# Shifted copies of a gated input for a 31-tap convolution: sixteen copies inside the core's memory a tile, or one store to device memory and four overlapping loads

## The chip, the cores and the metric

One core of one Trainium2 chip runs the whole program. Its engines are PE (TensorE, matrix products), DVE (VectorE), ACT (ScalarE), POOL (GpSimd) and SP (SyncE), each with its own queue, worked off in order; sixteen DMA engines move data for all of them. The metric is the device time of one execution in microseconds (us), lower is better.

## The reference

Two blocks follow each other: a conformer-like block with a recurrent branch and a pooling block, then a second block with chunked linear attention and a feed-forward part. Sequence length is 256, the width 1024, all in 32-bit floats. The change lies in the first block's convolution branch alone:

```python
def conformer_conv(va, vg, p):
    u = va * jax.nn.sigmoid(vg)
    u = depthwise_conv(u, p["conv_w"], p["conv_b"], CONV_PAD)      # 31 taps, padded 15 on each side
    return jax.nn.silu(layernorm(u, p["ln_g"], p["ln_b"]))

def even_mixer(h, h0, p):
    z = h @ p["w_in"]
    va, vg, ga, xb, gb = jnp.split(z, [W_CONV, 2 * W_CONV, 3 * W_CONV, 3 * W_CONV + W_LRU], axis=-1)
    y_a = conformer_conv(va, vg, p) * jax.nn.silu(ga)
    y_b, hT = rglru_branch(xb, p, h0, True)
    y_b = y_b * jax.nn.silu(gb)
    return jnp.concatenate([y_a, y_b], axis=-1) @ p["w_out"], hT
```

## The kernel before

Channels lie on the 128 partitions and time (256 steps) along the free dimension, so a tensor of width 1024 is eight tiles. All weights come as one stream of 512 KB tiles, in the order that `ORDER` lists (lines 49 to 74). A tile passes four stations. SP loads it into one of six buffers `raw` (L414), and to load tile n it waits until PE is done with tile n - 6. ACT rounds it to a high part `w_hi` (L866). DVE makes the rest, `w_lo` (L1230). PE multiplies in three products per 128 rows (L505 to L507), 24 instructions a tile. The tiles `gate` (recurrent gates) and `cv` (convolution) are used as they come, without ACT and DVE. ACT and DVE prepare weights at fixed places of their programs: ACT's `done(name, t)` first rounds everything up to four tiles ahead, and then waits for the named tile.

A second stream, `modw`, brings the modulation weights, 80 tiles of 512 KB, issued from POOL (L446) whenever DVE has used one of four buffers (L1264).

The stretch of the change is the first block's middle. For t = 0 to 7 PE makes `va t` and `vg t`; ACT copies `va` into the padded buffer `upad` (L919, three buffers) and writes the sigmoid of `vg` to `sg` (L924); DVE multiplies them in `gated(t)` (L1383). The convolution's 31 taps are then done on PE (L573) as 8 groups of 4 taps: the contraction runs over 32 channels times 4 taps. For that `shifts` (two buffers) has to hold, for each of four channel groups g, the 32 channels four times, on partitions 32 s to 32 s + 31 shifted by s steps. Between them PE runs the gates of the recurrent branch, `gates(head)` (L562). PE's order, with pieces of about equal weight, is: va 0, vg 0, gates 0, va 1, vg 1, gates 1, va 2, vg 2, conv 0, va 3, vg 3, conv 1, gates 2, va 4, vg 4, gates 3, conv 2, va 5, vg 5, conv 3, gates 4, va 6, vg 6, gates 5, conv 4, va 7, vg 7, conv 5, ga 0, ga 1, conv 6, gates 6, ga 2, ga 3, gates 7, conv 7, ga 4 to ga 7, statistics. In the order of the weight stream one `gate` tile serves two heads: gate 1 (heads 2 and 3) stands after vg 4, gate 2 after vg 6, gate 3 after ga 3.

ACT has one more thing to do here: `exps_of(p)` (L958, L962), twelve instructions on end for two heads, during which it rounds no weights. SP's queue interleaves the shifted copies with the weight stream: after the weight tile n is issued, and if tile n - 6 is a `vg t`, the sixteen copies of t follow, and only then the next weight tile.

Of the kernel before, what the change touches and what calls it, by code (L numbers as in the profile page):

```python
# [19 lines left out]
F32 = mybir.dt.float32  # L20
# [5 lines left out]
P = 128  # L26
D = 1024
T = 256
KT = D // P
RING = 6  # L30
# [18 lines left out]
def tiles_in_order():  # L49
    order = [("xb", t) for t in range(KT)]  # L50
    order += [("va", 0), ("vg", 0), ("va", 1), ("vg", 1), ("gate", 0), ("va", 2), ("vg", 2), ("cv", 0)]
    order += [("va", 3), ("vg", 3), ("cv", 1), ("va", 4), ("vg", 4), ("gate", 1), ("cv", 2)]
    order += [("va", 5), ("vg", 5), ("cv", 3), ("va", 6), ("vg", 6), ("gate", 2), ("cv", 4)]
    order += [("va", 7), ("vg", 7), ("cv", 5), ("ga", 0), ("ga", 1), ("cv", 6), ("ga", 2), ("ga", 3), ("gate", 3)]
    order += [("cv", 7)] + [("ga", t) for t in range(4, KT)] + [("gb", t) for t in range(KT)]
    for m in range(0, KT, 4):
        order += [("ya", t) for t in range(m, m + 4)] + [("yb", t) for t in range(m, m + 4)]
    order += [("ou", t) for t in range(2 * KT)] + [("og", t) for t in range(2 * KT)]
    order += [("grp", t) for t in range(KT)]
    for m in range(0, KT, 4):  # L60
        order += [("oa", t) for t in range(m, m + 4)] + [("ob", t) for t in range(m, m + 4)]
    order += [("f", t) for t in range(2 * HEADS)] + [("i", t) for t in range(HEADS)] + [("q", t) for t in range(HEADS)]
    order += [(n, t) for n in ("u", "v", "o") for t in range(HEADS)]
    order += [(n, t) for n in ("ga2", "gb2") for t in range(KT)]
    order += [(n, t) for t in range(HEADS) for n in ("pa", "pb")]
    order += [("wo", t) for t in range(KT)]
    order += [(n, t) for t in range(FT) for n in ("ua", "ub")]
    order += [(n, t) for t in range(KT) for n in ("d0", "d1", "d2")]
    return order


ORDER = tiles_in_order()
# [79 lines left out]
def build(nc, ins, out):  # L152
    with ExitStack() as ctx:
        base = nc.sbuf_base + (-nc.sbuf_base) % 32

        def at(name, kib, shape, dt=F32):
            return nc.alloc_sbuf_tensor_at(name, [P] + shape, dt, offset=base + int(kib * 1024))

        def sem(name):
            return ctx.enter_context(nc.semaphore(name))  # L160
# [27 lines left out]
        def columns(n):  # L188

            used[0] += n  # L190
            assert used[0] <= 448
            return small[:, used[0] - n:used[0]]
# [16 lines left out]
        UW = T + CONV_TAPS + 1  # L209
        RW = T + CONV_TAPS - 3  # L210
        shifts = [at("shifts0", W + 16, [4, RW]), at("shifts1", W + 32, [4, RW])]
        sg = at("sg", W + 20.5, [3, T])
        upad = at("upad", W + 36.5, [3, UW])
# [102 lines left out]
        h_ready = sem("h_ready")  # L316
        u_ready = sem("u_ready")
        u_gated = sem("u_gated")
        shifts_in = [sem(f"shifts_in{j}") for j in range(2)]
        ya_raw, ya_rounded, ya_ready = sem("ya_raw"), sem("ya_rounded"), sem("ya_ready")  # L320
        yb_raw, yb_rounded, yb_ready = sem("yb_raw"), sem("yb_rounded"), sem("yb_ready")
# [49 lines left out]
        lb_t = [columns(2 * HEADS) for _ in range(3)]  # L371
        lb, oml, noml = (columns(2 * HEADS) for _ in range(3))

        block = ctx.enter_context(nc.Block())


        def psum_of(name, t):

            return ps[PLACE[(name, t)][0]]
# [6 lines left out]
        def free_of(name, t):  # L386

            return ps_free[PLACE[(name, t)][0]]


        @block.sync
        def _(sp):
            sp.dma_start(ccs, ins["c_cols"]).then_inc(in_cc, 16)
            sp.dma_start(ctxT[:], ins["ctxT"]).then_inc(in_ctx, 16)
            sp.dma_start(x[:], ins["xT"]).then_inc(in_x, 16)
            sp.dma_start(cols[:], ins["cols"]).then_inc(in_con, 16)
            for k in range(KT):
                sp.dma_start(m0[:, k, :], ins["mod0_w"][k]).then_inc(mod0_in[k], 16)

            def shifted_copies(t):  # L400

                sp.wait_ge(u_gated, t + 1)
                if t >= 2:
                    sp.wait_ge(tile_done, TILE[("cv", t - 2)] + 1)
                for g in range(4):
                    for s in range(4):
                        sp.dma_start(shifts[t % 2][32 * s:32 * s + 32, g, :],  # L407
                                     upad[32 * g:32 * g + 32, t % 3, s:s + RW]).then_inc(shifts_in[t % 2], 16)

            def weights(first, end):  # L410
                for n in range(first, end):
                    if n >= RING:
                        sp.wait_ge(tile_done, n - RING + 1)
                    sp.dma_start(raw[n % RING][:], ins["stream"][n]).then_inc(raw_in[n % RING], 16)  # L414
                    if n >= RING and ORDER[n - RING][0] == "vg":
                        shifted_copies(ORDER[n - RING][1])

            weights(0, 4)
            sp.dma_start(con[:], ins["con"]).then_inc(in_con2, 16)
            sp.dma_start(c_row[:, 1, :], ins["c_rows"][0:1, :].partition_broadcast(P)).then_inc(in_crow, 16)  # L420
            weights(4, TILE[("ou", 0)] + RING)
            sp.wait_ge(prod_ready, KT)
            for n in (1, 2):
                sp.dma_start(c_row[:, 2 * n - 2, :], ins["c_rows"][n:n + 1, :].partition_broadcast(P)).then_inc(in_crow2, 16)
            weights(TILE[("ou", 0)] + RING, TILE[("og", 0)] + RING)
            sp.dma_start(ctx2T[:], ins["ctx2T"]).then_inc(in_ctx2, 16)
            weights(TILE[("og", 0)] + RING, TILE[("f", 0)] + RING)
            sp.dma_start(wsT[:], ins["wsT"]).then_inc(in_sgu, 16)
            sp.dma_start(bsr[0:1, :], ins["b_s"]).then_inc(in_sgu, 16)
            sp.dma_start(tri[:], ins["tri"]).then_inc(in_sgu, 16)  # L430
            weights(TILE[("f", 0)] + RING, NTILES)
            for k in range(KT):
                sp.wait_ge(stored, k + 1)
                sp.dma_start(out[:, k, :], x[:, k, :]).then_inc(out_done, 16)
            sp.wait_ge(out_done, 16 * KT)
# [14 lines left out]
        def _(pe):  # L450
# [22 lines left out]
            def weights(name, t):  # L473

                n = TILE[(name, t)]
                pe.wait_ge(raw_in[n % RING], 16 * (n // RING + 1))
                return raw[n % RING]

            def bank_of(name, t):

                bank, before = PLACE[(name, t)]
                if before:
                    pe.wait_ge(ps_free[bank], before)
                return ps[bank]
# [81 lines left out]
            def convolve(t):  # L566

                w, o = weights("cv", t), bank_of("cv", t)
                pe.wait_ge(shifts_in[t % 2], 256 * (t // 2 + 1))
                for n in range(QUADS):  # L570
                    for g in range(4):
                        c = slice(32 * g, 32 * g + 32)
                        mm = pe.matmul(o[c, 0:T], w[:, n, c], shifts[t % 2][:, g, 4 * n:4 * n + T], start=(n == 0),  # L573
                                       stop=(n == QUADS - 1))
                mm.then_inc(tile_done, 1)
# [8 lines left out]
            gates(1)  # L584
            va_vg(2)
            convolve(0)
            va_vg(3)
            convolve(1)
            gates(2)
            va_vg(4)  # L590
            gates(3)
            convolve(2)
            va_vg(5)
            convolve(3)
# [259 lines left out]
        def _(act):  # L854
# [14 lines left out]
            def done(name, t):  # L869

                highs(*ORDER[min(TILE[(name, t)] + RING - 2, NTILES - 1)])
                act.wait_ge(tile_done, TILE[(name, t)] + 1)
# [42 lines left out]
            def va_vg_out(t):  # L915
                done("va", t)
                if t >= 3:
                    act.wait_ge(shifts_in[(t - 3) % 2], 256 * ((t - 3) // 2 + 1))
                act.activation(upad[:, t % 3, CONV_LEFT:CONV_LEFT + T], psum_of("va", t)[:, 0:T], ACT.Copy) \  # L919
                   .then_inc(free_of("va", t), 1)  # L920
                done("vg", t)
                if t >= 3:
                    act.wait_ge(u_gated, t - 2)
                act.activation(sg[:, t % 3, :], psum_of("vg", t)[:, 0:T], ACT.Sigmoid).then_inc(free_of("vg", t), 1)  # L924
# [39 lines left out]
            def roots(p):  # L964
                for head in (2 * p, 2 * p + 1):
                    act.wait_ge(prod_ready, head + 1)
                    r = lr[:, PAIR_BUF[p] + head % 2]
                    act.activation(r, r, ACT.Sqrt).then_inc(root_ready, 1)

            va_vg_out(0)  # L970
            sigmoids(0)
            va_vg_out(1)
            sigmoids(1)
            va_vg_out(2)
            exps_of(0)
            conv_out(0)
# [1029 lines left out]
```

## Time and profile before

| | us |
|---|---|
| median of 3 runs | 1072.86 |
| lowest, highest | 1071.97, 1073.68 |
| the profiled execution | 1070.74 |
| its span, first to last instruction | 1068.9 |
| PE busy | 938.7 (88%) |
| PE weight loads busy | 867.8 (81%) |
| DVE busy | 709.9 (66%) |
| ACT busy | 503.7 (47%) |
| DMA: mean rate | 183 GB/s |
| shifted copies: issues, KB each | 128, 35.5 |

The busy shares are averages over the whole span. The stretch in which the shifted copies are issued runs from about 90 to 214 us, and the rows further down are read there. A stall is the idle time of an engine just before an instruction, and the profile names what ended it.

### The profile page before, as it was taken

Reading aid. Unit: us, or ns where it says so; the run is one execution under the profiler, and the core shown is the slowest. Engines: PE = TensorE matmul, PEld = TensorE weight load, DVE = VectorE, ACT = ScalarE, POOL = GpSimd, SP = SyncE. Lnnn points to the kernel's source line nnn. Section 1 sums busy time; section 2 is a strip of 40 time slices with the busy share of each in tenths; the row PEclk is TensorE's granted clock in tenths of the full one; section 3 lists DMA queues with packets and bytes.
Section 4 is the critical chain, followed back from the end, with each engine's and each line's share of the span. In section 5 each row is a group of like instructions: output and inputs, shape, how many; then the busy total and the mean of one; then the engine's idle time right before and its main releaser. Section 6 shows DMA issues by size and latency. Waiting matters only on the chain.

```text
span 1068.9 us, 17178 instructions
## 1 busy us (share of the span) xinstructions
PE 938.7 (88%) x7056; PEld 867.8 (81%) x7056; DVE 709.9 (66%) x1057; ACT 503.7 (47%) x725; POOL 42.5 (4%) x84
## 2 busy tenths in 40 slices
PE   5799698587799899897997898986989979999996
PEld 3588465457799899886997898986979979999996
DVE  3986647745955599977748796545458587566553
ACT  3634766667645554225334356446242445444441
POOL 0001000100000000100001200000000000000000
PEclk9799898798899899998999898997988989999998
DMA  9737756752456368874724954432334646666661
GB/s 378 287 103 222 243 171 227 254 193 82 119 178 195 140 182 289 286 248 141 275 94 180 356 177 121 132 118 60 99 99 123 177 156 202 189 180 181 194 201 57
DMA packets 57920, 195.27 MB, mean 183 GB/s; under 512 B 7921, under 2 KB 13169, under 8 KB 56434
## 3 DMA queue, kind: packets, MB, share of 16 engines
q1 hardware_dynamic: 46322, 152.23, 44.1%
q0 software_dynamic: 11520, 41.95, 11.5%
q8 instruction: 56, 0.92, 0.4%
q14 instruction: 22, 0.18, 0.0%
HBM read 188.44 MB, written 1.05 MB: 177 GB/s over the span
## 4 chain that ended last, share of the span: by engine, by line
PE 53%; DVE 19%; DMA 11%; ACT 7%; SPq 6%; issue 4%; DVEq 0%; ACTq 0%
PE ps L505 15%; PE ps L506 14%; PE ps L507 14%; SPq L407 6%; DVE w_lo L1230 5%; DMA raw<-in_stream 5%; DMA modw<-in_mod_w 4%; PE px L562 3%; ACT w_hi L866 2%; DMA m<-in_mod_w 2%; DVE modw L1264 2%; PE px L469 2%; DVE dump L1585 1%; DVE t L1250 1%; PE ps L573 1%
## 5 line engine op out<-in xcount | busy, mean ns | idle before, releaser
L1230 DVE TENSOR_TENSOR w_lo<-raw,w_hi 128x1024 fp32r<-128x1024 f32 x232 | 280.1, 1223 | 181.0 <-ACT w_hi L866 180.5
L866 ACT ACTIVATE w_hi<-raw 128x1024 fp32r<-128x1024 f32 x232 | 243.5, 1055 | 170.5 <-DMA raw<-in_stream 170.4
L505 PE MATMUL ps<-h_hi,w_hi 128*128 128x256 f32 (+1 forms) x928 | 280.3, 302 | 44.7 <-DVE w_lo L1230 29.6
L506 PE MATMUL ps<-h_lo,w_hi 128*128 128x256 f32 (+1 forms) x928 | 275.2, 297 | 0.0
L507 PE MATMUL ps<-h_hi,w_lo 128*128 128x256 f32 (+1 forms) x928 | 275.0, 296 | 0.0
L505 PEld LDWEIGHTS ps<-h_hi,w_hi 128*128 128x128 f32 x928 | 183.9, 198 | 54.8 <-DVE w_lo L1230 35.6
L506 PEld LDWEIGHTS ps<-h_lo,w_hi 128*128 128x128 f32 x928 | 184.0, 198 | 3.9 <-issue 1.2
L507 PEld LDWEIGHTS ps<-h_hi,w_lo 128*128 128x128 f32 x928 | 183.5, 198 | 2.6
L505 PE MATMUL ps<-h2o_hi,w_hi 128*128 128x256 f32 x352 | 107.0, 304 | 29.4 <-DVE w_lo L1230 13.0
L507 PE MATMUL ps<-h2o_hi,w_lo 128*128 128x256 f32 x352 | 104.1, 296 | 0.0
L506 PE MATMUL ps<-h2o_lo,w_hi 128*128 128x256 f32 x352 | 104.0, 296 | 0.0
L505 PEld LDWEIGHTS ps<-h2o_hi,w_hi 128*128 128x128 f32 x352 | 72.1, 205 | 32.0 <-DVE w_lo L1230 14.0
L1264 DVE SCALAR_TENSOR_TENSOR modw<-modw,c_row 128x1024 f32<-128x1024 f32 x64 | 76.2, 1223 | 16.9 <-DMA modw<-in_mod_w 16.8
L446 POOL DMA_DIRECT2D modw<-in_mod_w x80 | 42.3, 530 | 829.5 <-DVE modw L1264 557.8
L506 PEld LDWEIGHTS ps<-h2o_lo,w_hi 128*128 128x128 f32 x352 | 72.2, 205 | 0.3 <-issue 0.2
L507 PEld LDWEIGHTS ps<-h2o_hi,w_lo 128*128 128x128 f32 x352 | 72.1, 205 | 0.0
L562 PE MATMUL px<-xpad,raw 128*128 128x512 f32 x64 | 35.1, 699 | 17.4 <-DMA raw<-in_stream 17.4
L505 PE MATMUL ps<-ff_hi,w_hi 128*128 128x256 f32 x176 | 49.8, 283 | 0.0
L506 PE MATMUL ps<-ff_lo,w_hi 128*128 128x256 f32 x176 | 49.8, 283 | 0.0
L507 PE MATMUL ps<-ff_hi,w_lo 128*128 128x256 f32 x176 | 49.8, 283 | 0.0
L1041 ACT ACTIVATE sq<-x 128x256 f32<-128x256 f32 x32 | 13.4, 417 | 74.2 <-DVE x L1538 74.2
L562 PEld LDWEIGHTS px<-xpad,raw 128*128 128x128 f32 x64 | 13.8, 226 | 34.2 <-DMA raw<-in_stream 18.9
(301 smaller groups left out, 1730.8 us busy)
## 6 DMA issues: line engine op xcount, KB each, us to landing
raw<-in_stream SPq DMA_DIRECT2D x252, 512.0 KB, 3.7
modw<-in_mod_w POOLq DMA_DIRECT2D x80, 512.0 KB, 6.0
m<-in_mod_w SPq DMA_DIRECT2D x8, 1024.0 KB, 16.2
shifts<-upad SPq DMA_DIRECT2D x128, 35.5 KB, 3.7
c_row<-in_c_rows SPq DMA_DIRECT2D x3, 512.0 KB, 6.5
ctxT<-in_ctxT SPq DMA_DIRECT2D x1, 1024.0 KB, 4.9
x<-in_xT SPq DMA_DIRECT2D x1, 1024.0 KB, 7.0
ctx2T<-in_ctx2T SPq DMA_DIRECT2D x1, 1024.0 KB, 6.8
```

What stands on the lines that cost most here:

```text
L407: sp.dma_start(shifts[t % 2][32 * s:32 * s + 32, g, :], upad[32 * g:32 * g + 32, t % 3, s:s + RW]).then_inc(shifts_in[t % 2], 16)
L446: pool.dma_start(modw[j][:], ins["mod_w"][t]).then_inc(modw_in[j], 16)
L469: last = pe.matmul(bank[:, 0:T], ones, squares(k), start=(k == 0), stop=(k == tiles - 1))
L505: pe.matmul(o, wh, hi, start=start, stop=False)
L506: pe.matmul(o, wh, lo, start=False, stop=False)
L507: return pe.matmul(o, wl, hi, start=False, stop=stop)
L562: mm = pe.matmul(px[b][:, :], w[:, 4 * e + b, :], xpad[:, head, :, SCONV_LEFT:SCONV_LEFT + T], start=True, stop=True)
L573: mm = pe.matmul(o[c, 0:T], w[:, n, c], shifts[t % 2][:, g, 4 * n:4 * n + T], start=(n == 0), stop=(n == QUADS - 1))
L866: act.activation(w_hi[split[0] % HI_RING][:], raw[n % RING][:], ACT.Copy).then_inc(w_hi_ready, 1)
L1041: act.activation(dst[:, t, :], x[:, t, :], ACT.Square).then_inc(sq_ready, 1)
L1230: v.tensor_tensor(w_lo[n % RING][:], raw[n % RING][:], w_hi[split[0] % HI_RING][:].bitcast(F32), ALU.subtract).then_inc(w_lo_ready, 1)
L1264: v.scalar_tensor_tensor(out=modw[s][:], in0=modw[s][:], scalar=1.0, in1=c_row[:, row, :], op0=ALU.mult, op1=ALU.mult, accum_out=mod[:, t: ...
```

## The change

For each tile t the gated input is stored once, from `upad` to a new tensor `u_rows` in device memory, 128 rows of 288 values. Four loads then fill `shifts`: load g writes all 128 partitions of group g from a source pattern that counts 4 shifts (step 1 element), 32 rows (step 288) and 284 elements. The store stands on SP's queue where the sixteen copies stood. The loads stand two weight tiles later and wait for the store's landing, and as before for the convolution that read the buffer last. PE waits for 64 instead of 256 on the landing semaphore. ACT, before it overwrites an `upad` buffer, now waits for the store and not for the shifted copies. Bytes read per tile stay at 16 x 35.5 KB; 144 KB of store are added.

```diff
+            def store_u(t):
+
+                sp.wait_ge(u_gated, t + 1)
+                sp.dma_start(u_rows.ap()[t], upad[:, t % 3, :]).then_inc(u_stored[t], 16)
+
             def shifted_copies(t):
 
-                sp.wait_ge(u_gated, t + 1)
+                sp.wait_ge(u_stored[t], 16)
                 if t >= 2:
                     sp.wait_ge(tile_done, TILE[("cv", t - 2)] + 1)
                 for g in range(4):
-                    for s in range(4):
-                        sp.dma_start(shifts[t % 2][32 * s:32 * s + 32, g, :],
-                                     upad[32 * g:32 * g + 32, t % 3, s:s + RW]).then_inc(shifts_in[t % 2], 16)
+                    sp.dma_start(shifts[t % 2][:, g, :],
+                                 bass.AP(u_rows, (t * P + 32 * g) * UW, [[1, 4], [UW, 32], [1, RW]])) \
+                      .then_inc(shifts_in[t % 2], 16)
...
                     if n >= RING and ORDER[n - RING][0] == "vg":
-                        shifted_copies(ORDER[n - RING][1])
+                        store_u(ORDER[n - RING][1])
+                    if n >= RING + 2 and ORDER[n - RING - 2][0] == "vg":
+                        shifted_copies(ORDER[n - RING - 2][1])
...
-                pe.wait_ge(shifts_in[t % 2], 256 * (t // 2 + 1))
+                pe.wait_ge(shifts_in[t % 2], 64 * (t // 2 + 1))
...
                 if t >= 3:
-                    act.wait_ge(shifts_in[(t - 3) % 2], 256 * ((t - 3) // 2 + 1))
+                    act.wait_ge(u_stored[t - 3], 16)
```

SP's queue before, at the copies of tiles 0 and 1 (`raw` are weight tiles, the number after it the buffer):

```order
L407 DMA shifts_97<-upad 32x284 [waits u_gated]
L407 DMA shifts_97<-upad 32x284 x15
L414 DMA raw_53<-in_stream 128x1024 [waits tile_done]
L414 DMA raw_54<-in_stream 128x1024 [waits tile_done]
L407 DMA shifts_98<-upad 32x284 [waits u_gated]
L407 DMA shifts_98<-upad 32x284 x15
L414 DMA raw_49<-in_stream 128x1024 [waits tile_done]
L414 DMA raw_50<-in_stream 128x1024 [waits tile_done]
```

The same place of SP's queue after the change:

```order
L406 DMA u_rows<-upad 128x288 [waits u_gated]
L422 DMA raw_53<-in_stream 128x1024 [waits tile_done]
L422 DMA raw_54<-in_stream 128x1024 [waits tile_done]
L406 DMA u_rows<-upad 128x288 [waits u_gated]
L414 DMA shifts_97<-u_rows 128x1x284 [waits u_stored0]
L414 DMA shifts_97<-u_rows 128x1x284 x3
L422 DMA raw_49<-in_stream 128x1024 [waits tile_done]
```

The loads of tile 0 have moved behind two weight tiles and behind the store of tile 1, which waits for `gated(1)`.

SP's queue before, at the copies of tile 3 and what stands around them:

```order
L414 DMA raw_54<-in_stream 128x1024 [waits tile_done]
L407 DMA shifts_98<-upad 32x284 [waits tile_done,u_gated]
L407 DMA shifts_98<-upad 32x284 x15
L414 DMA raw_49<-in_stream 128x1024 [waits tile_done]
L414 DMA raw_50<-in_stream 128x1024 [waits tile_done]
L414 DMA raw_51<-in_stream 128x1024 [waits tile_done]
L407 DMA shifts_97<-upad 32x284 [waits tile_done,u_gated]
```

And after, from the store of tile 3 to the store of tile 4:

```order
L406 DMA u_rows<-upad 128x288 [waits u_gated]
L422 DMA raw_49<-in_stream 128x1024 [waits tile_done]
L422 DMA raw_50<-in_stream 128x1024 [waits tile_done]
L414 DMA shifts_98<-u_rows 128x1x284 [waits tile_done,u_stored3]
L414 DMA shifts_98<-u_rows 128x1x284 x3
L422 DMA raw_51<-in_stream 128x1024 [waits tile_done]
L406 DMA u_rows<-upad 128x288 [waits u_gated]
```

The weight tiles for gate 1 (stream number 21) and gate 2 (28), which stood right behind a block of sixteen copies, now stand ahead of the loads of their turn; right behind a block of loads stand now, among others, va 6 (number 26, here `raw_51`) and ga 0 (33). The order of PE, ACT and DVE is unchanged.

## Rows read from the trace of the kernel before

**Rows 1.** Page, shares of the chain that ended last, by engine
```profile
PE 53%; DVE 19%; DMA 11%; ACT 7%; SPq 6%; issue 4%; DVEq 0%; ACTq 0%
```

**Rows 2.** PE in order of time: start, us, line, operation [idle before, releaser]
```profile
98.51 3.60 PE L562 MATMUL px<-xpad,raw 128*128 128x512 f32 x8
107.79 0.42 PE L573 MATMUL ps<-shifts,raw 128*32 128x256 f32 x4
129.67 1.22 PE L562 MATMUL px<-xpad,raw 128*128 128x512 f32 x1 [8.10 <-DMA raw<-in_stream]
164.41 1.22 PE L562 MATMUL px<-xpad,raw 128*128 128x512 f32 x1 [6.35 <-DMA raw<-in_stream]
205.04 0.58 PE L505 MATMUL ps<-h_hi,w_hi 128*128 128x256 f32 x1 [11.77 <-DVE w_lo L1230]
219.55 1.97 PE L562 MATMUL px<-xpad,raw 128*128 128x512 f32 x2 [2.99 <-DMA raw<-in_stream]
252.24 0.58 PE L505 MATMUL ps<-h_hi,w_hi 128*128 128x256 f32 x1 [5.69 <-DVE w_lo L1230]
```

**Rows 3.** SP's DMA issues in order of time, 90 to 214 us: start, us
```profile
90.71 10.19 SPq L407 DMA_DIRECT2D shifts<-upad  x16
100.94 1.05 SPq L414 DMA_DIRECT2D raw<-in_stream  x2
114.71 10.93 SPq L407 DMA_DIRECT2D shifts<-upad  x16
125.68 1.53 SPq L414 DMA_DIRECT2D raw<-in_stream  x3
193.85 2.82 SPq L414 DMA_DIRECT2D raw<-in_stream  x4
```

**Rows 4.** Chain that ended last, 60 to 270 us: pieces, start and us
```profile
129.67 6.01 PE px L562 x8
141.42 3.44 PE px L562 x8
144.86 3.63 PE ps L573 x64
```

**Rows 5.** Instructions on `shifts`: duration of an issue, min/median/max ns; then landing
```profile
L407 SPq DMA_DIRECT2D shifts<-upad x128: 507/591/1318, 90.7 to 213.3; - x128
DMA to landing us min/median/max: 1.8/3.7/6.3
```

**Rows 6.** By stretch: us, PE, PEld, DVE, ACT, POOL busy, PEclk, DMA share, GB/s
```profile
100.00:110.00 10.00, 10.00 (x97) 7.80 (x99) 5.42 (x9) 4.73 (x8) 2.11 (x4) 1.00 1.04 342
120.00:130.00 10.00, 1.90 (x33) 0.99 (x24) 6.35 (x8) 8.56 (x11) 0.00 (x0) 0.71 0.44 128
180.00:190.00 10.00, 9.24 (x112) 7.57 (x108) 7.83 (x13) 8.90 (x13) 2.11 (x4) 1.00 0.97 365
```

**Rows 7.** Landing of the weight tiles `raw` issued from 95 to 240 us
```profile
DMA to landing us min/median/max: 3.5/5.9/9.4
```

**Rows 8.** ACT and DVE in order of time: start, us, operation [idle before, releaser]
```profile
106.36 1.06 ACT L866 ACTIVATE w_hi<-raw 128x1024 fp32r<-128x1024 f32 x1 [3.52 <-DMA raw<-in_stream]
149.80 1.06 ACT L866 ACTIVATE w_hi<-raw 128x1024 fp32r<-128x1024 f32 x1 [0.75 <-DMA raw<-in_stream]
158.95 1.33 ACT L962 ACTIVATE lr<-lr,small 128x512 f32<-128x512 f32 x2
99.19 0.43 DVE L1383 TENSOR_TENSOR upad<-upad,sg 128x256 f32<-128x256 f32 x1 [2.80 <-ACT sg L924]
166.60 2.35 DVE L1230 TENSOR_TENSOR w_lo<-raw,w_hi 128x1024 fp32r<-128x1024 f32 x2
```

**Rows 9.** POOL's issues of modulation tiles: start, us [idle before, releaser]
```profile
102.19 0.53 POOL L446 DMA_DIRECT2D modw<-in_mod_w  x1 [4.98 <-DVE modw L1264]
178.29 0.53 POOL L446 DMA_DIRECT2D modw<-in_mod_w  x1 [38.09 <-DVE modw L1264]
```

## What the change does to the time: the prediction

> **What bounds the kernel now.** First the page's chain: over the whole span PE holds 53% of it, and SP's queue 6%, an odd place for a queue that only issues [rows 1]. The copies are all issued between 90 and 214 us, so the rest is read there. Second, PE in order of time: up to 107.79 us it does not pause, and conv 0 starts then with no wait. Then come five stalls of more than 1 us, of 8.10, 6.35, 11.77, 2.99 and 5.69 us, 34.9 together [rows 2]. Third, SP's own order: a block of sixteen copies takes 10.2 to 10.9 us of issuing, eight blocks in all, and the next weight tile goes out only then [rows 3]. The two views fit: gate 1 goes out at 125.68, behind the block of 114.71 [rows 3], and PE starts on it at 129.67 [rows 2]. The stalls of 6.35 and 2.99 are gate 2 and gate 3 in the same position. The stall of 11.77 ends by way of DVE, but starts the same way: ga 1, first behind the block of tile 6, goes out at 193.85 [rows 3]; ACT has to round it before the sigmoid of vg 7, and DVE gates before it makes ga 0's low part. So SP's issuing sets the pace in four of five stalls. Each also costs clock: the granted clock falls from 1.00 to 0.71 in the stretch of the first [rows 6], which is part of the time at 1.2 GHz and not 2.4, and the gates after it take 6.01 us where they take 3.44 at full clock [rows 4]. About 2 us more for each of five stalls.
>
> **What is removed.** Sixteen issues of 0.63 us (10.19/16, median 0.59 alone) [rows 3, 5] become a store and four loads: 5 x 0.63 = 3.2 us. SP gains 7 us eight times, 55 us in all, but only stalls count. Heads 2, 4 and 6 no longer wait for a gate tile right behind the block; the three gate tiles now stand ahead of the loads of their turn: minus 8.10, 6.35 and 2.99, **-17.4 us**.
>
> **What is added, and what one tile's loads cost the DMA engines.** No row shows a store of this kind here; its landing lies between that of a copy, 1.8 us at best, and a weight tile's 5.9 in the middle [rows 5, 7]. Two weight tiles stand between it and the loads, each issued when PE is done with a tile, 2.92 us apart (va 2 and vg 2 run from 98.51 + 3.44 to 107.79 [rows 2, 4]), so the landing is covered by 5.8 us, at nothing; with no cover it would be 1.8 to 5.9 us a tile. SP's wait for the gated input stands where it stood. ACT's wait for the store comes due earlier than the one it replaces: nothing.
>
> The loads are the dispute. No row shows a load whose two sides count differently; each old copy has 32 rows on both sides and lands in 1.8 to 6.3 us [rows 5]. The new source counts 4, then 32, then 284; the target counts 128. I take it that a transfer is dealt out over the DMA engines by the outer count of both sides, which only 4 divides here, so that four of the sixteen engines carry all four loads, while every weight tile needs all sixteen. The price comes from rows: with all engines busy they move 342 GB/s (share 1.04) or 365 GB/s (share 0.97) [rows 6], 20.6 to 23.5 GB/s each. A load has 145 KB, 36.4 KB an engine, 1.55 to 1.77 us; four take **6.2 to 7.1 us** of those four engines, against 1.6 to 1.7 spread over all. A weight tile behind them waits that long.
>
> The Trainium skill, DMA: Bandwidth & Descriptors, section "Why a DMA increments its semaphore by 16 and not by 1", says the number of engines is the largest up to 16 that divides both patterns' slowest counts, and that the lowest-numbered are used: four here, the same four each time. No row of this case shows it. The same page's "Rules for kernel authors" would have small transfers coalesced, since under 64 KB one mostly pays overhead; by that alone the change would do what the first rival says.
>
> **Conv 0.** The lead was large: copies from 90.71, conv at 107.79. Now the store of tile 1 stands ahead, and waits for gated(1), 99.19 + 0.43 [rows 8], so the loads go out from 99.7. At that place the engines are full (share 1.04 for 10 us [rows 6]); a weight tile issued at 100.94 is taken up at 106.36 [rows 3, 8], 5.4 us against 3.5 at best [rows 7]. Landing is at least 99.7 + 5.4 + 6.2 = 111.3, 3.5 late. POOL issues four modulation tiles from 102.19 [rows 9]; 512 KB each, 32 KB an engine, about 1.5 us, served between the loads: up to 6 us more; with two weight tiles still in the backlog, 3 us, some 14 late. I take **+11**, near the upper end, because nothing on those engines is idle there.
>
> **Later convolutions.** The loads of t go out when the second tile after vg t is done. To conv t that leaves PE's work in between, with 2.9 us a weight tile, 3.6 a convolution and 3.44 gates [rows 4]: 12 us for t = 1, 19 for 2, 16 for 3, 22 for 4, 16 for 5, 15 for 6, 19 for 7. The landing needs 3.5 + 6.6 = 10 us alone, and as much as 22 with eight modulation tiles in between, which POOL issues from 178.29 on [rows 9], eight within 14 us, at t = 5. So conv 5 is some 8 us late, conv 3 about 1: **+9**, between 0 and 14.
>
> **Weight tiles behind the loads.** va 6 is right behind the loads of 3. Before, it was rounded at 149.80 after 0.75 us of waiting [rows 8], so it has no slack. ACT's exponentials follow at once and end at 160.3 (158.95 + 1.33), then the next tile's rounding, the sigmoid, the gating, and only at 166.60 comes DVE's low part of va 6 [rows 8]. A tile later by 6.6 us (11 with modulation tiles) moves this whole chain. Without the stall at 164.41 PE would want va 6 at 164.41 - 6.35 + 3.6 = 161.7 [rows 2, 4], and the chain without waiting gives about 165: 3.3 + 6.6 = 9.9 at least, less the 1 us lost at conv 3: **+9**. ga 0, behind the loads of 5, is in that place again; its 11.77 stays, take **-1**. At the last stall, of 5.69, the same happens in small: **+3**. Clock: five long stalls before, five after (conv 0, va 6, conv 5, ga 0, ga 7), so 0, within 4.
>
> **Sum.** -17.4 + 11 + 9 + 9 - 1 + 3 = +13.6. Against the profiled execution, 1070.74, that is 1084.3; against the median shown, 2.1 above it, 1086.4. Forecast **1086 us**, by itself between 1080 and 1093.
>
> **Rival 1, the loads spread over all sixteen engines** (or the source is dealt out by rows). Then four loads take 1.7 us and block nobody. For it: every row of a transfer here shows wide spreading. Against it: none of those has a source like this one. The 17.4 goes; conv 0 is still late by the moved issue, about 5 (111.3 - 6.2 + 1.7 = 106.8, plus modulation tiles); the exponentials on ACT, 9 us without rounding, leave va 6 a new stall of 5 (3.3 by the chain above, and a landing 2 later) and ga 0 one of 5 in place of 11.77; four long stalls and not five cost 2 us less clock: -17.4 + 5 + 5 - 6.8 - 2 = -16: 1057, from 1048 to 1066. It decides from the point where a block of loads costs a weight tile behind it less than the 7 us that SP saves.
>
> **Rival 2, the four engines are slower still.** The sources start at odd elements, 1136 bytes long, and between two queues a short piece may be served in turn with a 4 KB one. At 9 us a block and not 6.6, each of conv 0, conv 3, va 6, conv 5 and ga 0 loses 2.4 more: +12: 1098, to 1104.
>
> **Rival 3, four engines, but no collision with the modulation tiles.** Conv 0 is then 6.5 late (111.3 and 3 of backlog), the later ones 2 together, va 6 as worked out: -17.4 + 6.5 + 2 + 9 - 1 + 3 = +2: 1075, from 1071 to 1080.
>
> **How the numbers follow.** Forecast 0.62, rival 2 0.15, rival 3 0.10, rival 1 0.13. The likeliest gives 1086. The range takes the forecast, rival 2 and the upper part of rival 3, 1073 to 1104; what is left out is rival 1 and a few hundredths of rival 3, under 2 in 10. A measurement of this kernel can tell about 0.2%, 2.1 us, from no change. Slower by more is the forecast, rival 2 and half of rival 3, 0.82. Within it: the lower half of rival 3, 0.05. Faster: 0.13.
>
> **What would show it.** In the changed kernel's profile: conv 0 (L583 there) preceded by a stall of 4 to 14 us released by `shifts<-u_rows`; landing of these loads 8 to 22 us, not 4 to 6; weight tiles behind them landing after 10 and more; the issues of loads about 0.6 us each; gates 2 and 4 with no stall of several us before them; a DMA share in the stretch of 100 to 240 us of 0.6 or less while weights are late, since twelve engines idle. Loads landing within 5 us would prove rival 1 and the prediction wrong. If an issue takes over 2 us, SP is again the bound, and the sum has the wrong term.

## The result: slower by half a per cent, inside the range, with a sum more than twice too large

| | before | after |
|---|---|---|
| median of 20 runs, us | 1071.21 | 1075.10 |
| lowest, highest | 1066.52, 1073.68 | 1072.35, 1080.83 |
| span of the profiled execution | 1068.9 | 1071.7 |
| ratio, 95% interval | | 1.0048, 1.0035 to 1.0062 |
| SP's issues for the shifted copies | 128 | 8 stores and 32 loads |

The forecast was 1086, +13.6 us. The measured change is +5.1 by the ratio (3.7 to 6.6): the way forecast, inside the range, but well under half the size.

The page of after, its first line, the packets and the chain that ended last. SP's queue holds 2% of the chain where it held 6% [rows 1]; DMA's share grows from 11% to 14%:

```profile
span 1071.7 us, 17090 instructions
DMA packets 57151, 196.44 MB, mean 183 GB/s; under 512 B 6129, under 2 KB 12401, under 8 KB 55666
PE 53%; DVE 18%; DMA 14%; ACT 8%; issue 5%; SPq 2%; DVEq 0%; ACTq 0%
```

PE of after in order of time (start, us, line, operation [idle before, releaser]), the answer to [rows 2]:

```profile
117.25 1.08 PE L583 MATMUL ps<-shifts,raw 128*32 128x256 f32 x8 [10.41 <-DMA shifts<-u_rows]
157.68 0.66 PE L583 MATMUL ps<-shifts,raw 128*32 128x256 f32 x4 [3.53 <-DMA shifts<-u_rows]
173.79 0.58 PE L515 MATMUL ps<-h_hi,w_hi 128*128 128x256 f32 x1 [7.21 <-DVE w_lo L1240]
194.82 2.37 PE L583 MATMUL ps<-shifts,raw 128*32 128x256 f32 x40
210.28 0.58 PE L515 MATMUL ps<-h_hi,w_hi 128*128 128x256 f32 x1 [11.80 <-DVE w_lo L1240]
258.15 0.58 PE L515 MATMUL ps<-h_hi,w_hi 128*128 128x256 f32 x1 [10.71 <-DVE w_lo L1240]
```

The three stalls at the gates are gone. Conv 0 waits 10.41, conv 3 3.53, va 6 7.21; ga 0 still waits 11.80, conv 5 (194.82) does not wait at all.

SP's issues of after in order of time, against [rows 3]. The rows with x4 are blocks of loads; they take from 2.2 to 7.3 us, where four issues of 0.63 us would be 2.5:

```profile
99.00 3.86 SPq L414 DMA_DIRECT2D shifts<-u_rows  x4
102.91 7.45 SPq L422 DMA_DIRECT2D raw<-in_stream  x2
110.40 7.28 SPq L414 DMA_DIRECT2D shifts<-u_rows  x4
140.99 2.33 SPq L414 DMA_DIRECT2D shifts<-u_rows  x4
143.37 0.54 SPq L422 DMA_DIRECT2D raw<-in_stream  x1
196.75 6.51 SPq L414 DMA_DIRECT2D shifts<-u_rows  x4
```

The issues on `shifts` in ns (min/median/max), against [rows 5], and those of the weight tiles from 95 to 240 us, which took at most 1.17 us in before:

```profile
L414 SPq DMA_DIRECT2D shifts<-u_rows x32: 510/538/4820, 99.0 to 218.7; - x32
L422 SPq DMA_DIRECT2D raw<-in_stream x30: 327/431/6688, 94.8 to 238.7; - x30
```

And the landing of weight tiles issued from 95 to 240 us, against [rows 7]: the median went from 5.9 to 9.9 us.

```profile
DMA to landing us min/median/max: 3.6/9.9/15.3
```

SP also waits, from 88 to 240 us, for the landing of five of the eight stores, although two weight tiles stand between each store and its loads (us in total, times, longest):

```profile
SPq L414 <- DMA u_rows<-upad: 23.8, 5, 10.4
```

### The profile page after: what moved, and what is told of

It reads as the page before. It is cut to its first block, busy times and chain, and to the rows that moved or that the text cites. A ratio compares the mean times of both kernels' runs of the same rounds, so it can differ in the third digit from the quotient of the medians.

```text
span 1071.7 us, 17090 instructions
## 1 busy us (share of the span) xinstructions
PE 936.5 (87%) x7056; PEld 867.3 (81%) x7056; DVE 709.7 (66%) x1057; ACT 503.5 (47%) x725; POOL 42.7 (4%) x84
## 2 busy tenths in 40 slices
DMA packets 57151, 196.44 MB, mean 183 GB/s; under 512 B 6129, under 2 KB 12401, under 8 KB 55666
## 4 chain that ended last, share of the span: by engine, by line
PE 53%; DVE 18%; DMA 14%; ACT 8%; issue 5%; SPq 2%; DVEq 0%; ACTq 0%
PE ps L515 16%; PE ps L516 15%; PE ps L517 15%; DMA raw<-in_stream 6%; DVE w_lo L1240 5%; DMA modw<-in_mod_w 4%; DMA m<-in_mod_w 2%; ACT w_hi L876 2%; DVE modw L1274 2%; PE px L479 2%; SPq L414 2%; DMA u_rows<-upad 2%; DVE dump L1595 1%; DVE t L1260 1%; PE ps L650 1%
## 5 line engine op out<-in xcount | busy, mean ns | idle before, releaser
L515 PE MATMUL ps<-ff_hi,w_hi 128*128 128x256 f32 x176 | 49.8, 283 | 0.0
L516 PE MATMUL ps<-ff_lo,w_hi 128*128 128x256 f32 x176 | 49.8, 283 | 0.0
L517 PE MATMUL ps<-ff_hi,w_lo 128*128 128x256 f32 x176 | 49.8, 283 | 0.0
L583 PE MATMUL ps<-shifts,raw 128*32 128x256 f32 x512 | 32.2, 408 | 13.9 <-DMA shifts<-u_rows 13.9
L515 PE MATMUL ps<-y_hi,w_hi 128*128 128x256 f32 x128 | 37.2, 290 | 3.5 <-DVE w_lo L1240 3.5
```

The source lines that it names most:

```text
L515: pe.matmul(o, wh, hi, start=start, stop=False)
L516: pe.matmul(o, wh, lo, start=False, stop=False)
L517: return pe.matmul(o, wl, hi, start=False, stop=stop)
```

## How many engines carry a load

The trace names no DMA engine, but it counts packets. The page of before has this line:

```profile
DMA packets 57920, 195.27 MB, mean 183 GB/s; under 512 B 7921, under 2 KB 13169, under 8 KB 56434
```

Packets under 512 B fell by 7921 - 6129 = 1792. I take it that every engine which works on a transfer adds one small packet when it is done; no record says so, but all the counts below come out by it. If each of the 128 old copies and of the 8 stores used 16, then 128 x 16 = 2048 went, 8 x 16 = 128 came, and the 32 loads brought 2048 - 128 - 1792 = 128: four each. That is what the prediction assumed. By the Trainium skill's rule (DMA: Bandwidth & Descriptors, "Why a DMA increments its semaphore by 16 and not by 1") it has to be four; the trace agrees, with 128 small packets for 32 loads. The next experiments change this number and little else.

**Channels outside (sixteen engines).** `shifts` holds its rows channel by channel, and the weight tile of the convolution is laid out to match; the same four loads then count 32 outside.

```diff
-                                 bass.AP(u_rows, (t * P + 32 * g) * UW, [[1, 4], [UW, 32], [1, RW]])) \
+                                 bass.AP(u_rows, (t * P + 32 * g) * UW, [[UW, 32], [1, 4], [1, RW]])) \
...
-    blocks = np.zeros((KT, 4, 32, QUADS, 4, 32), w.dtype)
+    blocks = np.zeros((KT, 32, 4, QUADS, 4, 32), w.dtype)
...
-    blocks[:, :, f, :, :, f] = taps.reshape(QUADS, 4, KT, 4, 32).transpose(4, 2, 1, 0, 3)
+    blocks[:, f, :, :, :, f] = taps.reshape(QUADS, 4, KT, 4, 32).transpose(4, 2, 1, 0, 3)
```

> The changed kernel with one thing altered: shifts holds its rows channel by channel (partition 4 c + s) and not shift by shift (32 s + c); the convolution's weight tile is laid out to match. The four loads then count 32 rows outside and 4 shifts inside; their number, bytes, place in SP's queue and the store stay. Theory (a load runs on as many engines as divide the outer counts of both sides: 4 before, 16 now): conv 0's stall falls from 10.4 us to 0 to 6, the stalls at va 6 and ga 0 fall to about 5 each, no stall at conv 3, SP's issues of loads never exceed 1 us, 12 more small semaphore packets a load (384 in all: 1136-byte packets stay 4096), time 10 to 20 us under the kernel before: 1050 to 1061. Rival (the detour through device memory and the late place are what costs, not the number of engines): within 3 us of the changed kernel, 1072 to 1078.

Measured: 1045.37 us, ratio 0.9750 (0.9693 to 0.9807), 26 us below before, 30 below the changed kernel and 5 below the expected range. The page's packets, the issues in ns, and PE's waits from 95 to 270 us (in total, times, longest):

```profile
DMA packets 57535, 196.44 MB, mean 188 GB/s; under 512 B 6513, under 2 KB 12785, under 8 KB 56050
```

```profile
L414 SPq DMA_DIRECT2D shifts<-u_rows x32: 518/603/774, 100.5 to 194.0; - x32
```

```profile
PE ps L515 <- DVE w_lo L1240: 19.4, 5, 6.5
PE ps L583 <- DMA shifts<-u_rows: 2.7, 1, 2.7
```

384 small packets more than in the changed kernel, 12 a load, and not one of another size. Bytes, number, source, store and place are as in the changed kernel. Only the order of the rows differs as well, and the run with sixteen loads below, which keeps the old order, is faster too; so the 30 us hang on the number of engines. No issue takes over 0.78 us, where it was up to 4.82.

**Two engines.** Eight loads of 64 rows, 2 shifts outside.

```diff
-                    sp.dma_start(shifts[t % 2][:, g, :],
-                                 bass.AP(u_rows, (t * P + 32 * g) * UW, [[1, 4], [UW, 32], [1, RW]])) \
-                      .then_inc(shifts_in[t % 2], 16)
+                    for s in (0, 2):
+                        sp.dma_start(shifts[t % 2][32 * s:32 * s + 64, g, :],
+                                     bass.AP(u_rows, (t * P + 32 * g) * UW + s, [[1, 2], [UW, 32], [1, RW]])) \
+                          .then_inc(shifts_in[t % 2], 16)
```

> The changed kernel with eight loads of 64 rows, each with 2 shifts outside and 32 rows inside. Same bytes, same store, same place. Theory (the outer count gives the engines): two engines carry everything, 13 us a tile instead of 6.6; each load writes 2 semaphore packets, so 64 x 2 in all, the same 128 as with four loads of 4; conv 0's stall 15 to 18 us, stalls at nearly every convolution, 35 to 55 us over the kernel before: 1105 to 1127. Rival (rows are dealt out evenly whatever the pattern): near the changed kernel, plus 4 issues of 0.55 us a tile: 1075 to 1080.

Measured: 1117.77 us, ratio 1.0423 (1.0394 to 1.0452). PE's waits from 95 to 270 us, the issues, and the packets:

```profile
PE ps L584 <- DMA shifts<-u_rows: 43.0, 4, 15.9
PE ps L516 <- DVE w_lo L1241: 18.6, 4, 9.8
```

```profile
L415 SPq DMA_DIRECT2D shifts<-u_rows x64: 484/1246/5730, 100.4 to 263.8; - x64
```

```profile
DMA packets 57152, 196.45 MB, mean 176 GB/s; under 512 B 6129, under 2 KB 12401, under 8 KB 55666
```

The small packets are 6129 again: 64 loads bring what 32 brought, two each and not four. So the packets follow the outer count at 2, 4 and 16. The time lies in the theory's range here; with sixteen engines it lay below it. The median issue has more than doubled, to 1.25 us.

**Sixteen loads.** As many issues as before the change, from device memory, 32 rows outside on both sides.

```diff
-                    sp.dma_start(shifts[t % 2][:, g, :],
-                                 bass.AP(u_rows, (t * P + 32 * g) * UW, [[1, 4], [UW, 32], [1, RW]])) \
-                      .then_inc(shifts_in[t % 2], 16)
+                    for s in range(4):
+                        sp.dma_start(shifts[t % 2][32 * s:32 * s + 32, g, :],
+                                     bass.AP(u_rows, (t * P + 32 * g) * UW + s, [[UW, 32], [1, RW]])) \
+                          .then_inc(shifts_in[t % 2], 16)
```

> The changed kernel with sixteen loads of 32 rows from device memory instead of four of 128; both sides count 32 outside. Same bytes, same store, same place; SP issues 17 transfers a tile, as many as before the change plus one. Theory (what a load of four costs is its four engines): faster than the changed kernel although SP issues 7 us more a tile; conv 0's stall 2 to 6 us, no stalls at the gates, ga 0 near 9: 4 to 10 us under the kernel before, about 1064. Rival (device memory as source is slow, or SP's issue count is what matters): slower than the changed kernel, 1078 or more.

Measured: 1062.51 us, ratio 0.9914 (0.9879 to 0.9948). PE's waits there, 95 to 270 us:

```profile
PE ps L516 <- DVE w_lo L1241: 23.8, 4, 10.0
PE ps L584 <- DMA shifts<-u_rows: 6.3, 1, 6.3
```

The page counts 8049 small packets, 1920 more than in the changed kernel: 128 loads at sixteen and not 32 at four. So the detour through device memory with the old number of issues is 9 us faster than the kernel before, and PE no longer waits for a gate tile, since these now stand ahead of the copies. Four loads on four engines lose more than the 11 to 12 issues saved.

## What the place and the detour cost

**Loads at once.** Both layouts were also run with the loads right behind their store: `RING + 2` and `RING - 2` become `RING` and `RING`.

```diff
-                    if n >= RING + 2 and ORDER[n - RING - 2][0] == "vg":
-                        shifted_copies(ORDER[n - RING - 2][1])
+                    if n >= RING + 0 and ORDER[n - RING - 0][0] == "vg":
+                        shifted_copies(ORDER[n - RING - 0][1])
```

> The changed kernel with the four loads right behind their store, not two weight tiles later; all else stays, four engines included. SP now waits for the store's landing with nothing in between. Theory (four engines): conv 0's stall falls from 10.4 to 5 to 8 us, since the loads leave some 5 us earlier, but the gate tiles stand behind the loads again and the stalls of gates 2 and 4 come back: 8 to 15 us over the changed kernel, about 1086. Rival (the late place is what costs): faster than the changed kernel, under 1070.

Measured with four engines: 1100.66 us, ratio 1.0250 (1.0204 to 1.0297), some 25 over the changed kernel, where 8 to 15 were expected. PE's waits, then SP's issues around the second store:

```profile
PE ps L515 <- DVE w_lo L1240: 22.0, 3, 14.5
PE px L572 <- DMA raw<-in_stream: 19.0, 3, 10.3
PE ps L583 <- DMA shifts<-u_rows: 7.6, 1, 7.6
```

```profile
103.16 0.43 SPq L406 DMA_DIRECT2D u_rows<-upad  x1
119.00 2.66 SPq L414 DMA_DIRECT2D shifts<-u_rows  x4
```

SP stands 15.4 us for one store's landing, behind the backlog of the four engines, and all weights stand behind SP. That is one of eight such waits, 49.8 us in all. The two weight tiles between store and loads cover a part of this in the changed kernel, where 23.8 us are left.

> The channel-by-channel loads on sixteen engines (the 1045 us version) with the loads right behind their store and not two weight tiles later. It shows what the place is worth when no engine is crowded. Theory: conv 0's stall of 2.7 us goes, but SP now waits about 2 us, and in crowded stretches 5, for each store's landing, and the gate tiles stand behind that: 3 to 8 us slower, 1048 to 1053. Rival (the store's landing is covered anyway): the same or up to 3 us faster.

Measured with sixteen engines: 1058.10 us, ratio 0.9891 (0.9867 to 0.9916), 13 over the version with the gap, where 3 to 8 were expected. PE's waits there:

```profile
PE ps L515 <- DVE w_lo L1240: 26.0, 6, 11.2
PE px L572 <- DMA raw<-in_stream: 6.7, 2, 4.6
```

Conv 0's wait is gone, as expected, and the gates' have come back; SP waits 32.2 us for stores, and 7.0 in the version with the gap. The late place is no fault of the change but its better half.

**No detour, four issues.** The kernel before, in the layout by channels, with four copies inside the core.

```diff
-                    for s in range(4):
-                        sp.dma_start(shifts[t % 2][32 * s:32 * s + 32, g, :],
-                                     upad[32 * g:32 * g + 32, t % 3, s:s + RW]).then_inc(shifts_in[t % 2], 16)
+                    sp.dma_start(shifts[t % 2][:, g, :],
+                                 bass.AP(upad, 32 * g * 3 * UW + (t % 3) * UW, [[3 * UW, 32], [1, 4], [1, RW]])) \
+                      .then_inc(shifts_in[t % 2], 16)
```

> The kernel before, with its copies inside the core's memory, but four a tile and not sixteen: shifts is held channel by channel (partition 4 c + s), so that one transfer of 128 rows counts 32 partitions of the gated input outside and 4 shifts inside. No store, no device memory, copies in their old place. Theory (SP's issuing is what the kernel before lost, and engines what the changed one lost): no stall at conv 0, none above 2 us at the gates, time at or below the 1045 of the channel-by-channel loads: 1039 to 1046. Rival (a source of 32 partitions read four times is slow, or the old place right behind the gating blocks SP): 1050 or more.

Measured: 1040.20 us, ratio 0.9745 (0.9706 to 0.9784). PE's waits from 95 to 270 us:

```profile
PE ps L505 <- DVE w_lo L1230: 18.3, 6, 6.5
```

No wait for a copy and none for a gate tile is left.

**Copies left out.**

```diff
-                for g in range(4):
+                for g in range(4 if t < 2 else 0):
...
-                pe.wait_ge(shifts_in[t % 2], 256 * (t // 2 + 1))
+                pe.wait_ge(shifts_in[t % 2], 256)
```

(ACT's wait is cut to the first 256 likewise. This kernel leaves out the copies of tiles 2 to 7, so its convolutions from tile 2 on read stale rows.)

> The kernel before with the shifted copies of tiles 2 to 7 left out; those of tiles 0 and 1 are made, and the later convolutions read what lies in the buffers (so the outputs of the convolution are those of stale rows). It gives the price of all that copying by any means. Theory: all that the copies cost on the kernel before is SP's issuing, so leaving six of eight out comes to the same time as four copies a tile on chip, within 4 us: 1038 to 1046. Rival (DMA traffic of the copies also costs): 5 us or more below the on-chip version with four.

Measured: 1040.91 us, ratio 0.9740 (0.9710 to 0.9771), the same as with four copies on chip. So the copying of tiles 2 to 7 costs nothing there beyond what these runs can tell, some 4 us; the kernel before paid about 30 us for it, in SP's issuing. What PE still waits for is the low parts (20.0 us, five times).

## Why 13.6 and not 5: two holds of the modulation tiles

**One hold.** POOL's third group waits for conv 0.

```diff
+                if n == 2 * MOD_SLOTS:
+                    pool.wait_ge(tile_done, TILE[("cv", 0)] + 1)
```

> The changed kernel with one more wait: POOL issues the third group of modulation tiles (the four that went out at 101 to 105 us, among the loads of tile 0) only when conv 0 is done. They are used some 30 us later. Theory of the prediction (half of conv 0's stall is modulation tiles served between the loads): conv 0's stall falls from 10.4 to between 4 and 7 us, and the time by 2 to 6 us against the changed kernel: 1069 to 1073. Rival (the stall is the four engines' own backlog of weights and loads): stall 9 to 11, time unchanged within 1 us.

Measured: 1074.62 us, ratio to before 1.0042 (1.0023 to 1.0060), the same as the changed kernel. The stalls of conv 0 and conv 3:

```profile
113.28 1.08 PE L585 MATMUL ps<-shifts,raw 128*32 128x256 f32 x8 [5.27 <-DMA shifts<-u_rows]
157.52 1.08 PE L585 MATMUL ps<-shifts,raw 128*32 128x256 f32 x8 [4.82 <-DMA shifts<-u_rows]
```

Half of conv 0's stall was modulation tiles, as the prediction had it: 10.41 to 5.27. But little of the 5 us is left by conv 3, which starts at 157.52 and not 157.68. (PE comes to the gates before va 2 at 98.66 in this trace and at 97.49 in after, so counted from there 1.3 us are left at conv 3, 1.2 at va 6, and 2.9 at the statistics after ga 7, which start at 261.68 and not 263.41.) Most of the stall saved was not time saved. The medians differ by 0.5 us and their intervals leave room for some 2 more; the expectation of the time failed.

The chain that ended last shows why. In the changed kernel it has no piece of PE between 106.86 and 173.79 us: the stalls of conv 0 and conv 3 are not on it. It goes over SP's long issues to a weight tile that ACT has to round before it goes on to tile 3, over the store of tile 3 and its loads to the tile of va 6, and over ACT's exponentials to PE. Its main pieces up to there (start, us), in after and with one hold:

```profile
106.86 2.74 SPq L422
113.39 2.85 SPq L414
117.72 10.41 DMA raw<-in_stream
131.77 9.21 DMA u_rows<-upad
143.37 15.27 DMA raw<-in_stream
```

```profile
115.81 9.69 DMA u_rows<-upad
132.28 10.12 DMA u_rows<-upad
144.11 4.13 SPq L414
148.29 10.34 DMA raw<-in_stream
```

**Two holds.** The fourth group, too, waits, for conv 3.

```diff
+                if n in (2 * MOD_SLOTS, 3 * MOD_SLOTS):
+                    pool.wait_ge(tile_done, TILE[("cv", 0 if n == 2 * MOD_SLOTS else 3)] + 1)
```

> The changed kernel with two waits on POOL: the third group of modulation tiles as in the run before this one (held until conv 0 is done), and also the fourth, which there went out from 140 to 144 us among the loads of tile 3 and the weight tile of va 6; it is now held until conv 3 is done. Theory (stalls add up, as the prediction's sum has it; the first hold's gain was eaten by the next collision): conv 3's stall of 4.8 us goes, va 6's of 6.8 falls to about 3, the time drops by 5 to 8 us against 1074.6, to 1067 to 1070. Rival (what is won ahead is lost again in the chain from a late weight tile over ACT's exponentials to ga 0, so stalls don't add up): conv 3's stall goes, but ga 0's and va 6's grow, time within 2 us of 1074.6.

Measured: 1070.06 us, ratio to before 0.9989 (0.9977 to 1.0001), 5 us faster than the changed kernel (6 by the two ratios to before). Conv 3 no longer waits; va 6 does:

```profile
169.39 0.58 PE L517 MATMUL ps<-h_hi,w_hi 128*128 128x256 f32 x1 [7.64 <-DVE w_lo L1242]
```

The time is what the first theory gave, its stall at va 6 is not; the rival's stall at va 6 is there (it grew from 6.81 to 7.64), but ga 0's fell from 12.33 to 10.20, and its time is not there. What the traces do agree on is when ACT rounds the tile of va 6, the one behind the loads of tile 3. In after, with one hold and with two:

```profile
158.66 1.06 ACT L876 ACTIVATE w_hi<-raw 128x1024 fp32r<-128x1024 f32 x1 [12.82 <-DMA raw<-in_stream]
```

```profile
158.65 1.06 ACT L878 ACTIVATE w_hi<-raw 128x1024 fp32r<-128x1024 f32 x1 [11.37 <-DMA raw<-in_stream]
```

```profile
154.27 1.06 ACT L878 ACTIVATE w_hi<-raw 128x1024 fp32r<-128x1024 f32 x1 [6.63 <-DMA raw<-in_stream]
```

One hold leaves this moment where it was to 0.01 us (counted from the gates before va 2, it comes 1.2 sooner); two move it by 4.4 us, and PE's start of va 6 by as much (173.79 to 169.39). Here the chain does pass the loads of tile 0 and conv 0:

```profile
102.39 10.68 DMA shifts<-u_rows
145.03 9.21 DMA raw<-in_stream
```

Of the 4.4 us, 3.3 are SP's: without modulation tiles among them the loads of tile 3 take 2.20 us to issue and not 5.82, and va 6's tile goes out at 145.03 and not 148.29; the rest is a shorter landing. An explanation that fits: up to there the four engines are simply full, and what counts is what they have to carry by then, not where it collides. The changed kernel by stretch (us, PE, PEld, DVE, ACT, POOL busy, PEclk, DMA share, GB/s):

```profile
92.00:159.00 67.00, 53.07 (x472) 40.37 (x474) 36.13 (x51) 33.92 (x49) 6.36 (x12) 0.91 0.74 238
160.00:178.00 18.00, 10.79 (x74) 7.05 (x67) 9.44 (x11) 17.82 (x25) 0.00 (x0) 0.78 0.48 133
```

67 us at 238 GB/s are 15.9 MB; the loads of tiles 0 to 3 are 2.3 of it, the rest, 13.6, is spread over sixteen, 0.85 MB each. Four engines have 0.85 + 0.58 = 1.43 MB in 67 us, 21.4 GB/s, within the 20.6 to 23.5 that an engine was worked out to move when all are full. The first hold moves a group of modulation tiles within this stretch, the second moves one out of it, into the 18 us in which ACT makes exponentials and the DMA engines have half their work (133 GB/s in after, and 136 from 160 to 175; the row of two holds, 160 to 175 us, has 267):

```profile
160.00:175.00 15.00, 7.36 (x41) 6.05 (x40) 10.84 (x12) 14.88 (x22) 0.79 (x2) 0.77 0.88 267
```

By this, 131 KB less on each of the four engines (four tiles of 512 KB, each dealt over sixteen) is an estimated 5.6 to 6.4 us; va 6 came 4.4 earlier. That the engines are the four crowded ones is worked out, not seen, since no record names an engine, and no run tests this sum by itself.

More of the change, by code:

```diff
@@ L318, in build @@
         u_gated = sem("u_gated")
+        u_stored = [sem(f"u_stored{t}") for t in range(KT)]
         shifts_in = [sem(f"shifts_in{j}") for j in range(2)]
@@ L372, in build @@
         lb, oml, noml = (columns(2 * HEADS) for _ in range(3))
+        u_rows = nc.dram_tensor("u_rows", (KT, P, UW), F32, kind="Internal")
         block = ctx.enter_context(nc.Block())
```

## The prediction, point by point

The steps that failed are three: the later convolutions, put at +9 and measured at 3.5; the store's landing and the length of an issue, put at nothing and at 0.6 us; and the adding up of stalls, of which some are not on the chain that ended last.

- **What bounds the kernel before: right.** SP's issuing was the bound, and more than the prediction said. It expected 7 saved us a tile to be worth 17.4, or 16 in rival 1 after all costs; with sixteen engines the gain was 26, on chip 31.
- **Removed, -17.4: right.** The three stalls at the gates are gone, and two of under 1 us (0.52 and 0.76, in the trace, not in the sum) shrank to one of 0.17.
- **Four engines: right**, by packets and by three runs with 16, 2 and 16.
- **Store covered, at nothing: failed.** Landing has a median of 8.4 us and up to 12.2, not 1.8 to 5.9, and two weight tiles do not cover that: SP stood 23.8 us in five waits. For tile 3 the second weight tile was out by 138.66 and the loads went out at 140.99, so 2.3 us of this wait lie on the chain to va 6, and 0.9 more at tile 7; the longest, 10.4 at tile 4, is not on it. With no cover at all the cost is some 25 us or 3.1 a tile, within the 1.8 to 5.9 that the prediction named for that case.
- **Conv 0, +11: right**, 10.41, and half of it by modulation tiles, as worked out.
- **Later convolutions, +9: failed, 3.5.** This is the largest mis-sized term. The step "eight modulation tiles in between ... at t = 5" took the place of those issues from the trace of before. In after only four (184 to 188 us) fell between the loads of tile 5 (179.63) and conv 5 (194.82, no wait); the next went out from 195.4. Conv 3 and not conv 5 was the late one.
- **va 6, +9: 7.2. ga 0, -1: 0.0. Last stall, +3: 5.0.** The chain over ACT's exponentials is there in each: the tile rounded at 158.66, PE at 173.79.
- **Sum.** By stalls after: -17.4 - 1.1 + 10.4 + 3.5 + 7.2 + 0.0 + 5.0 = +7.6. The statistics after ga 7 start 6.0 us later than in before (263.41 against 257.41), PE having come into the stretch 1 us sooner. The rest of the span is 808.3 us against 811.5. In the traces of the six kernels of the first comparison (before, after, and the four run together) it lies between 807.1 and 811.5 with nothing changed there, so the 3 us are no effect of the change that can be told. +6 in the stretch agrees with the 3.7 to 6.6 of all runs.
- **Why it came out more than twice too large.** 5.5 us lie in the later convolutions, 1.8 in va 6, 1.7 in conv 0 and the small stalls, less 2 in the last stall and 1 in ga 0. Behind them stands the way of summing: collisions were priced one by one, each at its worst moment, though several need not lie on one chain. The one-hold run shows this: taking 5.1 us off the first stall changed the time by less than the runs can tell. That a late conv 0 also gives the four engines time to clear their backlog is argued and not shown.
- **Signs named ahead.** Of "landing of these loads 8 to 22 us" nothing can be read: the trace has no landing for transfers on four engines. "Issues about 0.6 us" held for the median (0.54) and not for all: single ones pass the 2 us from which the prediction called SP the bound again, SP's issues are on the chain from 106.86 to 117.72 us, and the sum has no term for that. The conv 0 stall of 4 to 14 us, the gates without a stall and weight tiles landing after 10 us and more (15.27 for va 6) are there. A DMA share of 0.6 or less from 100 to 240 us is not: it is 0.73, against 0.67 in before and 0.53 with two engines. Why it is so high is open.
- **Rival 1** did not happen with this pattern; with the other it did, and by more than forecast: 1045 against 1057, range from 1048.
- **Rival 3** gave 1075, the time that was measured, but not for its reason: it had conv 0 late by 6.5 with no collision with modulation tiles, and conv 0 was late by 10.4, 5.1 of it by them. Its small price for the later convolutions, 2, was the nearer one (3.5).
- **Rival 2**, four slower engines, did not happen: no stall is above the forecast's but ga 0's, by 1 us, and the last.

## What to carry to other kernels

Before four transfers replace sixteen, look at the outer count of both access patterns: in these runs it, not the bytes, decided how many DMA engines worked, and reordering rows (with the matching order in the constant operand) can turn 4 engines into 16 at no cost. When issuing is the bound and everything lies on chip, fewer issues in the old place beat a detour whose landing has to be waited for. Where a few engines are full, add up what they must carry by the time that matters; stalls taken one by one are not a sum, and the chain that ended last tells which of them counts.

## What was not expected of the hardware

- SP's issue of a transfer is not a fixed 0.6 us: with loads on four engines single issues took up to 4.82 us and blocks of four up to 7.3, on two engines up to 5.73 and 1.25 in the median, and the same four loads on sixteen engines at most 0.78. Weight tiles behind the four-engine loads took up to 6.69 to issue, against 1.17 in before. Many small transfers on sixteen engines are not free of it either: the old copies took up to 1.32, the sixteen loads up to 1.56. So crowded DMA engines hold the issuing queue itself; that they do so by full queues is an inference.
- A store of 144 KB, among crowded engines, took 15.4 us from its issue until SP could go on, against 1.7 at best in after.
- 128 rows on chip, each of 32 partitions read four times with shifts of one element, land in 2.6 to 6.6 us: as good as the 32-row copies [rows 5], at a quarter of the issues.
